# An attention stage: a weight tile's rounding and a gate's silu moved ahead by one pair of heads

## The chip, the cores and the metric

The kernel runs on one core of a Trainium2 chip. The metric is the device time of one execution in microseconds (us); lower is better. The time before is the median of three executions.

## The reference

The whole program is a model of several mixers and feed-forward layers over 512 tokens of width 1024. What the change touches is the attention stage of the last block. It has six pairs of heads of width 64: three pairs of "forgetting" attention (fox) and three pairs of indexer-selected attention (dsa). Cut to what matters:

```
z = rmsnorm(x) @ w_in                      # q, k, v and gate columns of each head
fox:  s = q.k * scale + F[t] - F[s], causal mask;    o = softmax(s) @ v;  out = o * silu(gate)
dsa:  s = q.k * scale over the top 128 keys of an indexer's score;  o = softmax(s) @ v;  out = o * silu(gate)
x = x + concat(mixers) @ w_out;  final rmsnorm
```

## The kernel before, in words

All work is done transposed: features lie on the partitions, 512 tokens along the free axis. A product in full precision is made of three matmuls on rounded parts: a weight tile is split into a high part (ScalarE, `split_high`, L151, 128x1024) and a low part (here GpSimd, `split_low`, L160), and TensorE multiplies high by high, low by high and high by low (L187 to L189).

`attention` (L2840) runs the six pairs i = 0 to 5 (NP = 6, of them NF = 3 fox). TensorE works on two pairs at once: while it attends over pair i it projects pair i + 1, which has four weight tiles s = 0 to 3 (queries, keys, gate, values), each of eight steps of three matmuls. The order is written out by hand, one program for each engine, and semaphores join them:

- **TensorE**, `body(i)` (L2945): the eight steps of tile 0 of the next pair, the turn (transpose) of the values (L204), `scores(i, 2)` (L2910), then for each of the eight items n (a head and a block of 128 queries; items 0 and 1 are the longest, with 512 keys) three more steps of the projection, the transposes of the probabilities `turn(i, n)` (L2918), scores of items to come at n = 1 and 3, and `values(i, n - 1)` (L2929). Tile 1 is steps 8 to 15, in items 0 to 2; tile 2 begins with step 16. Before the first step of a tile PE waits for that tile's low part and for its bank to be free. In the last pair PE does steps of the output projection (`mix`) in their place.
- **ScalarE (ACT)**, `body(i)` (L2986): `exp(n)` (L2992), `divide(n)` (L2997), the copy of the transposed probabilities out of PSUM, `turn(n)` (L3004), and between them the rounding of weight tiles of the next pair: `high(i + 1, 1)` after `divide(0)`, tiles 2 and 3 at n = 2 and 3, tile 0 of the pair after next at n = 4. The silu of the gate (L3017) stands between `divide(1)` and `turn(0)`, with a load of the silu table in front and of the exp table behind it (L3018). Its result lies in one buffer, `gate`, so it waits until the previous pair's output is formed.
- **VectorE (DVE)**, `body(i)` (L3083): per item the logits (L3099) and their maximum (L3101), the reciprocal of the sum of the item before (`invert`, L3076), in the fox pairs also a part of the choice of the 128 keys (L2826), and the takes of finished projections out of PSUM (`take`, L3071): queries at n = 1, keys at n = 3, gate at n = 6, values at the next pair's start. `out` (L3081) multiplies the gate into the previous pair's output at n = 1. In pair 4 it also makes the low parts of the output projection's sources (`half.low`, L554), one per item from n = 3.
- **GpSimd (POOL)** makes the low part of each weight tile as soon as the high one is there. **SyncE (SP)** loads a tile when the low part of the tile before in the same slot is done.

In what follows "pair 1" is the second pair, and the copy of item n is `turn(n)` on ACT.

Of the kernel before, what the change touches and what calls it, by code (L numbers as in the profile page):

```python
# [14 lines left out]
F32 = mybir.dt.float32  # L15
F32R = mybir.dt.float32r
U32 = mybir.dt.uint32
ACT = mybir.ActivationFunctionType
AX = mybir.AxisListType.X

P = 128
T = 512
# [30 lines left out]
LNEXP = "natural_log_exp_and_others"  # L53
# [33 lines left out]
class Core:  # L87
# [30 lines left out]
    def sb(self, name, shape, dtype=F32):  # L118
        return self.stack.enter_context(self.nc.sbuf_tensor(name, shape, dtype))

    def sem(self, name):
        self.sems.append(self.nc.alloc_semaphore(name))
        return self.sems[-1]
# [109 lines left out]
class Opening:  # L233
# [10 lines left out]
    def high(self, act, m, lo=0, hi=T):  # L244
        k = self.k
        k.nc.scalar.activation(k.uh[:, m, lo:hi], k.x[:, m, lo:hi], ACT.Copy, scale=self.gain(m)).then_inc(self.u_high, 1)
# [2593 lines left out]
def attention(k, fox_weights, dsa_weights, half):  # L2840
# [4 lines left out]
    nc = k.nc  # L2845
    sem, sb = k.sem, k.sb
    NF, NI = HF // 2, 2 * NT
    NP = 2 * NF
    R = 4
    items = [(a, t) for t in reversed(range(NT)) for a in range(2)]  # L2850
    qs, ks = ([sb(f"a_{s}{i}", [P, T], F32) for i in range(2)] for s in ("q", "k"))
    v, vraw, gate, graw = (sb(f"a_{s}", [P, T], F32) for s in ("v", "v_raw", "gate", "g_raw"))
    L = sb("a_logits", [P, R, T], F32)
    PT = sb("a_probsT", [P, 2, T], F32)
    st = sb("a_stats", [P, NI, 4], F32)
    taken = [sem(f"a_{s}_taken") for s in ("q", "k", "g", "v")]
# [4 lines left out]
    b_s, b_t, b_o = k.ps[4:6], k.ps[6], k.ps[7]  # L2861
# [4 lines left out]
    def y_tile(i):  # L2866

        return k.y[:, 5 + i if i < NF else 2 + i - NF, :]

    with nc.Block() as block:  # L2870
# [109 lines left out]
        @block.scalar  # L2980
        def _(act):
            def high(i, s):
                k.wait_product(act, 4 * i + s - 4)
                k.split_high(act, s, i)

            def body(i):  # L2986
                nxt2, end = i < NP - 1, i == NP - 1

                def exp(n):
                    act.wait_ge(max_ready, NI * i + n + 1)  # L2990
                    l = L[:, n % R, 0:(items[n][1] + 1) * P]
                    nc.scalar.activation(l, l, ACT.Exp, bias=st[:, n, 0:1], accum_out=st[:, n, 1:2]).then_inc(exp_done, 1)  # L2992

                def divide(n):
                    act.wait_ge(inverted, NI * i + n + 1)
                    l = L[:, n % R, 0:(items[n][1] + 1) * P]
                    nc.scalar.activation(l, l, ACT.Copy, scale=st[:, n, 2:3]).then_inc(p_ready, 1)  # L2997

                def turn(n):
                    t = items[n][1]  # L3000
                    act.wait_ge(turned, NI * i + n + 1)
                    if i or n >= 2:
                        act.wait_ge(pv_done, NI * i + n - 1)
                    nc.scalar.activation(PT[:, n % 2, 0:(t + 1) * P], b_t[:, 0:(t + 1) * P], ACT.Copy).then_inc(pt_ready, 1)  # L3004
                exp(0)
                exp(1)
                divide(0)
                high(i + 1, 1)
                act.wait_ge(v_turned, i + 1)
                if i:  # L3010
                    act.wait_ge(pv_done, NI * i)
                nc.scalar.activation(v[:, :], k.ps[3][:, :], ACT.Copy).then_inc(v_copied, 1)
                divide(1)
                act.wait_ge(taken[2], i + 1)
                if i:
                    act.wait_ge(y_ready, i)
                nc.scalar.activation(gate[:, :], graw[:, :], ACT.Silu).then_inc(gate_done, 1)  # L3017
                nc.scalar.preload_act_table_set(LNEXP)  # L3018
                turn(0)
                for n in range(2, NI):  # L3020
                    exp(n)
                    if n > 2:
                        divide(n - 1)
                    if n in (2, 3):
                        high(i + 1, n)
                    if nxt2 and n == 4:
                        high(i + 2, 0)
                    if i == NP - 2 and n < 7:
                        half.high(act, n - 2)
                    elif end and n in (2, 4):  # L3030
                        if n == 2:
                            k.wait_product(act, 4 * NP - 1)
                        half.high(act, 4 + n // 2)
                    elif end and n >= 6:
                        half.wait_product(act, n - 6)
                        half.split_high(act, n - 2)
                    if n > 2:
                        turn(n - 2)
                divide(NI - 1)
                turn(NI - 2)  # L3040
                turn(NI - 1)
                if end:
                    half.wait_product(act, 2)
                    half.split_high(act, 6)

            high(1, 0)
            for i in range(NP):
                body(i)
            act.wait_ge(y_ready, NP)
            half.high(act, KD - 1)  # L3050
# [9 lines left out]
        @block.vector  # L3060
        def _(dve):
            raws = (qs, ks, (graw, graw), (vraw, vraw))

            def take(i, s):

                k.wait_product(dve, 4 * i + s)
                if i and s == 2:
                    dve.wait_ge(gate_done, i)
                if i and s == 3:
                    dve.wait_ge(v_turned, i)  # L3070
                nc.vector.tensor_tensor(raws[s][i % 2][:, :], k.ps[s][:, :], k.rn[:, :], ALU.mult).then_inc(taken[s], 1)  # L3071

            def invert(i, n):

                dve.wait_ge(exp_done, NI * i + n + 1)
                nc.vector.reciprocal(st[:, n, 2:3], st[:, n, 1:2]).then_inc(inverted, 1)  # L3076

            def out(i):
                dve.wait_ge(pv_done, NI * i + NI)
                dve.wait_ge(gate_done, i + 1)  # L3080
                nc.vector.tensor_tensor(y_tile(i), gate[:, :], b_o[:, :], ALU.mult).then_inc(y_ready, 1)  # L3081

            def body(i):  # L3083
                end, fox = i == NP - 1, i < NF
                take(i, 3)
                if i == NF:
                    choice.finish(dve)
                for n, (a, t) in enumerate(items):
                    w, g = (t + 1) * P, NI * i + n
                    dve.wait_ge(st_done, g + 1)  # L3090
                    if g >= R:
                        dve.wait_ge(turned, g + 1 - R)
                    l = L[:, n % R, 0:w]
                    if fox:
                        d = b_s[a][:, w - P:w]
                        nc.vector.tensor_tensor(d, d, k.c("causal"), ALU.add).then_inc(masked, 1)
                        dve.wait_ge(masked, g + 1)
                    b = k.fb[:, 2 * i + a, 0:w] if fox else k.bias[:, OFF[t]:OFF[t + 1]]
                    nc.vector.scalar_tensor_tensor(l, b_s[a][:, 0:w], DH ** -0.5, b, ALU.mult, ALU.add).then_inc(logits_ready, 1)  # L3099
                    dve.wait_ge(logits_ready, g + 1)  # L3100
                    nc.vector.tensor_reduce(st[:, n, 0:1], l, AX, ALU.max, negate=True).then_inc(max_ready, 1)  # L3101
                    if fox:
                        choice.some(dve, 2)
                    if n:
                        invert(i, n - 1)
                    if n == 1 and i:
                        out(i - 1)
                    if fox:
                        choice.some(dve, 2)
                    if i < NP - 1 and n in (1, 3, 6):  # L3110
                        take(i + 1, (1, 3, 6).index(n))
                    if i == NP - 2 and n > 2:
                        half.low(dve, n - 3)
                    elif end and n in (3, 5):
                        half.low(dve, 4 + n // 2)
                invert(i, NI - 1)

            for s in range(3):
                take(0, s)
            for i in range(NP):  # L3120
                body(i)
            out(NP - 1)
            half.low(dve, KD - 1)
    k.count({s: NP for s in range(4)})
# [152 lines left out]
```

## Time and profile before

| | |
|---|---|
| median of 3 executions | 1842.07 us (1835.05 to 1844.43) |
| the profiled execution's own time | 1838.89 us |
| its span, first to last instruction | 1837.0 us |
| PE (matmuls) busy | 1741.9 us, 95% of the span |
| PEld (weight loads) busy | 1395.7 us, 76% |
| DVE busy | 1090.7 us, 59% |
| ACT busy | 854.3 us, 47% |
| POOL busy | 428.8 us, 23% |

The table shows where an engine spent its time over the whole program; the attention stage is the stretch from 1568 to 1810 us of the span. PE stands for the matmuls and PEld for the weight loads that go before them on the same engine. A row's idle time is the time in which the engine had nothing running in front of that instruction, with the instruction that ended the wait. Matmul ends are modelled, so successive matmuls overlap in the rows; a start is read directly.

### The profile page before, as it was taken

Reading aid. Unit: us, or ns where it says so; the run is one execution under the profiler, and the core shown is the slowest. Engines: PE = TensorE matmul, PEld = TensorE weight load, DVE = VectorE, ACT = ScalarE, POOL = GpSimd, SP = SyncE. Lnnn points to the kernel's source line nnn. Section 1 sums busy time; section 2 is a strip of 40 time slices with the busy share of each in tenths; the row PEclk is TensorE's granted clock in tenths of the full one; section 3 lists DMA queues with packets and bytes.
Section 4 is the critical chain, followed back from the end, with each engine's and each line's share of the span. In section 5 each row is a group of like instructions: output and inputs, shape, how many; then the busy total and the mean of one; then the engine's idle time right before and its main releaser. Section 6 shows DMA issues by size and latency. Waiting matters only on the chain. (4 is left out here: it accounts for less than half of the span.)

```text
span 1837.0 us, 23870 instructions
## 1 busy us (share of the span) xinstructions
PE 1741.9 (95%) x8346; PEld 1395.7 (76%) x8346; DVE 1090.7 (59%) x1705; ACT 854.3 (47%) x1452; POOL 428.8 (23%) x332
## 2 busy tenths in 40 slices
PE   7998998999999999899999999999999989899997
PEld 5666887777888888777888877888888766666665
DVE  5544444567565643678788848666553476667243
ACT  5553455544333332456555645333332352445663
POOL 0342454211111100135546510111100111222222
PEclk9999999999999999999999999999999999999999
DMA  5111100232223222311222121322232320211121
GB/s 206 38 69 58 47 35 24 75 109 72 100 93 101 92 93 101 103 47 58 69 69 69 48 92 58 102 93 95 76 115 98 108 74 22 80 47 46 58 69 46
DMA packets 39904, 140.28 MB, mean 76 GB/s; under 512 B 4496, under 2 KB 4752, under 8 KB 39696
## 3 DMA queue, kind: packets, MB, share of 16 engines
q1 hardware_dynamic: 39824, 139.23, 22.5%
q8 instruction: 49, 0.80, 0.2%
q14 instruction: 31, 0.25, 0.0%
HBM read 137.11 MB, written 2.10 MB: 76 GB/s over the span
## 5 line engine op out<-in xcount | busy, mean ns | idle before, releaser
L187 PE MATMUL bank<-u_high,w_high 128*128 128x512 f32 x1580 | 650.4, 412 | 24.2 <-POOL w_low L160 9.9
L189 PE MATMUL bank<-u_high,w_low 128*128 128x512 f32 x1580 | 621.5, 393 | 0.0
L188 PE MATMUL bank<-u_low,w_high 128*128 128x512 f32 x1580 | 620.9, 393 | 0.0
L187 PEld LDWEIGHTS bank<-u_high,w_high 128*128 128x128 f32 x1580 | 300.5, 190 | 113.8 <-issue 37.5
L151 ACT ACTIVATE w_high<-w_ring 128x1024 fp32r<-128x1024 f32 x233 | 244.1, 1052 | 226.3 <-PE bank L189 172.7
L189 PEld LDWEIGHTS bank<-u_high,w_low 128*128 128x128 f32 x1580 | 299.3, 189 | 65.5
L188 PEld LDWEIGHTS bank<-u_low,w_high 128*128 128x128 f32 x1580 | 300.8, 190 | 58.3 <-issue 3.8
L160 DVE TENSOR_TENSOR w_low<-w_ring,w_high 128x1024 fp32r<-128x1024 f32 x176 | 221.0, 1258 | 178.9 <-ACT w_high L151 178.7
L160 POOL TENSOR_TENSOR w_low<-w_ring,w_high 128x1024 fp32r<-128x1024 f32 x57 | 135.7, 2390 | 544.3 <-ACT w_high L151 544.3
L881 ACT ACTIVATE conv_up<-bank,col_sb 128x512 f32<-128x512 f32 x88 | 68.6, 780 | 270.5 <-DVE bank L936 270.5
L996 POOL TENSOR_TENSOR hidden<-conv_up 128x512 f32 x44 | 58.2, 1323 | 494.0 <-DVE conv_up L947 373.7
L936 DVE TENSOR_TENSOR bank<-bank,root_in 128x512 f32<-128x512 f32 x88 | 61.4, 698 | 134.1 <-PE bank L189 133.5
L187 PE MATMUL bank<-src_high_down,w_high 128*128 128x512 f32 x352 | 137.3, 390 | 2.3 <-DVE src_low_down L479 2.3
L188 PE MATMUL bank<-src_low_down,w_high 128*128 128x512 f32 x352 | 136.9, 389 | 0.0
L189 PE MATMUL bank<-src_high_down,w_low 128*128 128x512 f32 x352 | 136.9, 389 | 0.0
L1319 POOL TENSOR_TENSOR c_X<-c_k,c_dif 128x256 f32<-128x256 f32 x56 | 59.4, 1060 | 149.9 <-ACT c_dif L1210 149.9
L187 PEld LDWEIGHTS bank<-src_high_down,w_high 128*128 128x128 f32 x352 | 66.1, 188 | 17.5 <-issue 2.2
L189 PEld LDWEIGHTS bank<-src_high_down,w_low 128*128 128x128 f32 x352 | 66.1, 188 | 13.7
L188 PEld LDWEIGHTS bank<-src_low_down,w_high 128*128 128x128 f32 x352 | 66.1, 188 | 13.6
L946 DVE SCALAR_TENSOR_TENSOR conv_up<-bank,col_sb,conv_up 128x511 f32<-128x511 f32 x88 | 65.9, 749 | 15.6 <-ACT conv_up L881 11.9
L947 DVE SCALAR_TENSOR_TENSOR conv_up<-bank,col_sb,conv_up 128x510 f32<-128x510 f32 x88 | 65.9, 748 | 10.1 <-DVE conv_up L946 0.3
L1354 DVE TENSOR_TENSOR c_dif<-c_G 128x512 f32<-128x512 f32 x56 | 54.5, 997 | 24.9 <-PE bank L1116 24.5
(414 smaller groups left out, 2320.8 us busy)
## 6 DMA issues: line engine op xcount, KB each, us to landing
w_ring<-ffn_up SPq DMA_DIRECT2D x88, 512.0 KB, 3.4
w_ring<-ffn_down SPq DMA_DIRECT2D x44, 512.0 KB, 3.4
w_ring<-c_in SPq DMA_DIRECT2D x32, 512.0 KB, 3.4
w_ring<-g_in SPq DMA_DIRECT2D x16, 512.0 KB, 3.9
w_ring<-m_in SPq DMA_DIRECT2D x12, 512.0 KB, 4.9
w_ring<-fox_in SPq DMA_DIRECT2D x12, 512.0 KB, 3.5
w_ring<-dsa_in SPq DMA_DIRECT2D x12, 512.0 KB, 3.4
w_ring<-ab_out SPq DMA_DIRECT2D x8, 512.0 KB, 4.7
```

The lines of the kernel that those rows point to most:

```text
L151: self.nc.scalar.activation(self.ws[s][0][:, :], self.w[:, s, :], ACT.Copy).then_inc(self.w_high, 1)
L160: eng.tensor_tensor(low[:, :], self.w[:, s, :], high[:, :].bitcast(F32), ALU.subtract).then_inc(self.w_split, 1)
L187: nc.tensor.matmul(out, a[0], b[0], start=start, stop=False)
L188: nc.tensor.matmul(out, a[0], b[1], start=False, stop=False)
L189: return nc.tensor.matmul(out, a[1], b[0], start=False, stop=stop)
L881: nc.scalar.activation(cg[:, s, :], bank(i, s)[:, :], ACT.Identity, bias=coef(4 * i + s, 3), scale=coef(4 * i + s, 2)).then_inc(tap_done, 1)
L936: nc.vector.tensor_tensor(bank(i, s)[:, :], bank(i, s)[:, :], k.rn[:, :], ALU.mult).then_inc(taken, 1)
L946: ch.link(nc.vector.scalar_tensor_tensor(cg[:, s, 1:T], bank(i, s)[:, 0:T - 1], coef(4 * i + s, 1), cg[:, s, 1:T], ALU.mult, ALU.add))
L947: nc.vector.scalar_tensor_tensor(cg[:, s, 2:T], bank(i, s)[:, 0:T - 2], coef(4 * i + s, 0), cg[:, s, 2:T], ALU.mult, ALU.add).then_inc(con ...
L996: nc.gpsimd.tensor_tensor(h[:, bass.ds(2 * i + s // 2, 1), :], cg[:, s - 1:s, :], cg[:, s:s + 1, :], ALU.mult).then_inc(mul_done, 1)
L1319: nc.gpsimd.tensor_tensor(x[:, :, 0, :], blocks(kk[:, :], b)[:, :, 0, :], d[:, :, 0, :], ALU.mult)
L1354: nc.vector.tensor_tensor(dif[:, l % R, :].rearrange("p (n b) -> p n b", b=2 * b), g, ref, ALU.subtract).then_inc(diff_ready, 1)
```

## The change

- ACT rounds tile 1 of the pair after next at n = 5, in the pair in front (`high(i + 2, 1)`), in place of `high(i + 1, 1)` in the pair itself; tile 1 of pair 1 is rounded before the loop. POOL and SP follow in the same order of tiles.
- The gate has two buffers. The silu of pair i + 1 with its two table loads stands at the end of pair i on ACT, behind the last copy; that of pair 0 before the loop.
- DVE takes the next pair's keys at n = 4 and not at n = 3.
- In pair 4 DVE's low parts begin at n = 4; the fifth follows the fourth at n = 7.

```diff
--- before.py
+++ after.py
@@ -2849,7 +2849,8 @@
     R = 4
     items = [(a, t) for t in reversed(range(NT)) for a in range(2)]
     qs, ks = ([sb(f"a_{s}{i}", [P, T], F32) for i in range(2)] for s in ("q", "k"))
-    v, vraw, gate, graw = (sb(f"a_{s}", [P, T], F32) for s in ("v", "v_raw", "gate", "g_raw"))
+    v, vraw, graw = (sb(f"a_{s}", [P, T], F32) for s in ("v", "v_raw", "g_raw"))
+    gates = [sb(f"a_gate{i}", [P, T], F32) for i in range(2)]
     L = sb("a_logits", [P, R, T], F32)
     PT = sb("a_probsT", [P, 2, T], F32)
     st = sb("a_stats", [P, NI, 4], F32)
@@ -2983,6 +2984,13 @@
                 k.wait_product(act, 4 * i + s - 4)
                 k.split_high(act, s, i)
 
+            def silu(i):
+                act.wait_ge(taken[2], i + 1)
+                if i > 1:
+                    act.wait_ge(y_ready, i - 1)
+                nc.scalar.activation(gates[i % 2][:, :], graw[:, :], ACT.Silu).then_inc(gate_done, 1)
+                nc.scalar.preload_act_table_set(LNEXP)
+
             def body(i):
                 nxt2, end = i < NP - 1, i == NP - 1
 
@@ -3005,17 +3013,11 @@
                 exp(0)
                 exp(1)
                 divide(0)
-                high(i + 1, 1)
                 act.wait_ge(v_turned, i + 1)
                 if i:
                     act.wait_ge(pv_done, NI * i)
                 nc.scalar.activation(v[:, :], k.ps[3][:, :], ACT.Copy).then_inc(v_copied, 1)
                 divide(1)
-                act.wait_ge(taken[2], i + 1)
-                if i:
-                    act.wait_ge(y_ready, i)
-                nc.scalar.activation(gate[:, :], graw[:, :], ACT.Silu).then_inc(gate_done, 1)
-                nc.scalar.preload_act_table_set(LNEXP)
                 turn(0)
                 for n in range(2, NI):
                     exp(n)
@@ -3023,8 +3025,8 @@
                         divide(n - 1)
                     if n in (2, 3):
                         high(i + 1, n)
-                    if nxt2 and n == 4:
-                        high(i + 2, 0)
+                    if nxt2 and n in (4, 5):
+                        high(i + 2, n - 4)
                     if i == NP - 2 and n < 7:
                         half.high(act, n - 2)
                     elif end and n in (2, 4):
@@ -3039,11 +3041,15 @@
                 divide(NI - 1)
                 turn(NI - 2)
                 turn(NI - 1)
+                if nxt2:
+                    silu(i + 1)
                 if end:
                     half.wait_product(act, 2)
                     half.split_high(act, 6)
 
             high(1, 0)
+            high(1, 1)
+            silu(0)
             for i in range(NP):
                 body(i)
             act.wait_ge(y_ready, NP)
@@ -3078,7 +3084,7 @@
             def out(i):
                 dve.wait_ge(pv_done, NI * i + NI)
                 dve.wait_ge(gate_done, i + 1)
-                nc.vector.tensor_tensor(y_tile(i), gate[:, :], b_o[:, :], ALU.mult).then_inc(y_ready, 1)
+                nc.vector.tensor_tensor(y_tile(i), gates[i % 2][:, :], b_o[:, :], ALU.mult).then_inc(y_ready, 1)
 
             def body(i):
                 end, fox = i == NP - 1, i < NF
@@ -3107,10 +3113,12 @@
                         out(i - 1)
                     if fox:
                         choice.some(dve, 2)
-                    if i < NP - 1 and n in (1, 3, 6):
-                        take(i + 1, (1, 3, 6).index(n))
-                    if i == NP - 2 and n > 2:
-                        half.low(dve, n - 3)
+                    if i < NP - 1 and n in (1, 4, 6):
+                        take(i + 1, (1, 4, 6).index(n))
+                    if i == NP - 2 and n > 3:
+                        half.low(dve, n - 4)
+                        if n == 7:
+                            half.low(dve, n - 3)
                     elif end and n in (3, 5):
                         half.low(dve, 4 + n // 2)
                 invert(i, NI - 1)
```

## Rows read from the trace of the kernel before

**Rows 1.** Windows, pair by pair from one scores(i, 2) to the next.
```profile
core 0: us, PE busy (x) PEld busy (x) DVE busy (x) ACT busy (x) POOL busy (x), PEclk, DMA share, GB/s
1579.99:1618.31 38.32, 35.20 (x177) 25.33 (x177) 27.49 (x82) 18.32 (x38) 9.38 (x4) 1.00 0.17 55
1618.31:1657.52 39.21, 35.18 (x178) 25.33 (x177) 29.19 (x87) 19.82 (x41) 9.44 (x4) 1.00 0.16 55
1657.52:1697.78 40.26, 36.21 (x177) 26.61 (x176) 27.62 (x80) 21.37 (x42) 10.25 (x5) 0.96 0.16 53
1697.78:1733.97 36.19, 34.99 (x177) 25.40 (x176) 11.43 (x30) 19.38 (x40) 9.83 (x5) 1.00 0.19 59
1733.97:1771.39 37.42, 34.02 (x171) 24.12 (x171) 17.54 (x34) 21.78 (x45) 8.31 (x4) 1.00 0.16 57
...
```

**Rows 2.** Waits of the stage: who for whom, us in total, times, longest.
```profile
PEld bank L187 <- POOL w_low L160: 15.6, 10, 3.9
...
DVE a_k L3071 <- PE bank L189: 14.3, 5, 3.5
...
PE bank L187 <- POOL w_low L160: 9.2, 6, 3.3
...
PE bank L2918 <- ACT a_probsT L3004: 7.4, 10, 1.9
```

**Rows 3.** Timeline of PE in pair 1: start, us, instruction, count [idle before it].
```profile
1618.31 0.92 PE L2910 MATMUL bank<-a_k,a_q 64*128 64x384 f32 x4
1622.51 0.50 PE L187 MATMUL bank<-u_high,w_high 128*128 128x512 f32 x1 [3.28 <-POOL w_low L160]
...
1624.71 0.60 PE L2918 MATMUL bank<-cst_sb,a_logits 128*128 128x128 f32 x4
...
1627.90 0.63 PE L2918 MATMUL bank<-cst_sb,a_logits 128*128 128x128 f32 x4 [0.50 <-ACT a_probsT L3004]
...
1631.82 0.51 PE L187 MATMUL bank<-u_high,w_high 128*128 128x512 f32 x1
...
1636.59 0.52 PE L2918 MATMUL bank<-cst_sb,a_logits 128*128 128x128 f32 x3 [0.19 <-ACT a_probsT L3004]
```

**Rows 4.** Timeline of ACT in pair 1.
```profile
1623.18 0.72 ACT L2997 ACTIVATE a_logits<-a_logits,a_stats 128x512 f32<-128x512 f32 x1 [2.67 <-DVE a_stats L3076]
...
1625.22 0.63 ACT L3017 ACTIVATE a_gate<-a_g_raw 128x512 f32<-128x512 f32 x1
1625.87 1.28 ACT L3018 ACT_TABLE_LOAD   x1
1627.16 0.60 ACT L3004 ACTIVATE a_probsT<-bank 128x512 f32<-128x512 f32 x1
...
1628.25 1.04 ACT L151 ACTIVATE w_high<-w_ring 128x1024 fp32r<-128x1024 f32 x1
```

**Rows 5.** Timeline of POOL (one row) and DVE in pair 1.
```profile
1620.11 2.35 POOL L160 TENSOR_TENSOR w_low<-w_ring,w_high 128x1024 fp32r<-128x1024 f32 x1 [20.84 <-ACT w_high L151]
...
1631.80 0.69 DVE L3071 TENSOR_TENSOR a_k<-bank,root_in 128x512 f32<-128x512 f32 x1 [2.08 <-PE bank L189]
```

**Rows 6.** Timeline of ACT where pairs meet: 1 to 2, and 3 to 4.
```profile
1652.92 0.72 ACT L2992 ACTIVATE a_logits<-a_logits,a_stats 128x512 f32<-128x512 f32 x1 [2.56 <-DVE a_stats L3101]
...
1729.01 0.73 ACT L2992 ACTIVATE a_logits<-a_logits,a_stats 128x512 f32<-128x512 f32 x1 [2.22 <-DVE a_stats L3101]
```

**Rows 7.** Timeline of POOL, DVE, ACT and PE in pair 4.
```profile
1744.95 2.37 POOL L160 TENSOR_TENSOR w_low<-w_ring,w_high 128x1024 fp32r<-128x1024 f32 x1 [0.18 <-ACT w_high L151]
...
1745.40 2.46 DVE L554 TENSOR_TENSOR mix_low<-y_mix,mix_high 128x512 fp32r<-128x512 f32 x1
...
1748.68 0.51 ACT L2992 ACTIVATE a_logits<-a_logits,a_stats 128x256 f32<-128x256 f32 x1 [2.81 <-DVE a_stats L3101]
...
1751.78 0.52 PE L2918 MATMUL bank<-cst_sb,a_logits 128*128 128x128 f32 x3 [1.95 <-ACT a_probsT L3004]
```

**Rows 8.** Windows, four us behind the longest wait, in pair 2.
```profile
1660.00:1664.00 4.00, 2.25 (x5) 1.82 (x6) 3.86 (x12) 1.76 (x2) 1.70 (x1) 0.71 0.28 97
```


## The prediction

> **What bounds the kernel.** The page gives PE 95% of the span, so I went to the stage that the change touches and cut it into pairs [rows 1]. From one `scores(i, 2)` to the next the first three pairs, fox, take 38.3, 39.2 and 40.3 us, and the next, dsa, 36.2, though PE is busy for about 35 us in each. PE sets the time, and what exceeds 35 us is mostly waits. The list of waits says which [rows 2]: matmuls waited 9.2 us in all, six times, for a weight tile's low part, and the transposes 7.4 us, ten times, for the copy of the item before out of PSUM. That is 16.6 us in a stage of 242.
>
> The timelines of pair 1 show where the two are made [rows 3 to 5]. PE ends its scores at 1619.2 and stands 3.28 us before step 8, because tile 1 was rounded by ACT only after `divide(0)`; POOL's part, 2.35 us, ended at 1622.46. The first copy (1627.16) stands behind the second divide and the gate's block, 1623.90 to 1627.16: a silu of 0.63 and two table loads of 1.28. Its transposes for item 1 waited for it 0.50 us more. The third piece is in pair 4 [rows 7]: a transpose waits 1.95 us, because ACT came late to `exp(4)` (2.81 us idle); the maximum before it stood on DVE behind the keys, for which DVE waits 14.3 us in five pairs [rows 2].
>
> **The change, part by part.**
>
> *Tile 1 a pair earlier.* Its 1.04 us on ACT [rows 4] and 2.35 us on POOL are done some 20 us before PE wants them: POOL had been idle for 20.84 us in front of that work [rows 5], so it has room. SP's load for the slot also goes out earlier. Step 8 then waits for nothing: the 9.2 us go. What ACT gains at the start of a pair it pays at n = 5, 1.04 us between `divide(4)` and the copy of item 3. The third part pays for that.
>
> *The gate's block.* 3.26 us leave the way of the first copy. In pair 1 that copy can start at 1623.18 + 0.67 = 1623.85, since `divide(1)` is held by DVE and not by PE [rows 4]. PE gets to it like this [rows 3]: scores end at 1619.2, three steps last 2.2 (1622.51 to 1624.71), the transposes and three steps more 2.7 (1624.71 to 1627.40), so it is there at 1624.1, and the copy ends near 1624.5. So about 0.4 us of wait stays in pair 1, and by the same path about 0.2 in pair 2. From the copy to step 16 lies a chain of exp, rounding of tile 2 and POOL's 2.35: 1627.16 to 1631.82, 4.66 us. It now starts at 1623.85 and ends at 1628.5, where PE would come at 1628.0. So step 16 is 3.3 us earlier than before, and not 3.8. In a dsa pair DVE has no choice of keys to make (busy 11.4 us against 27 to 29 [rows 1]), and I find no wait there.
>
> The block itself now stands between the last copy of a pair and the next `exp(0)`, where ACT had idled 2.56 us between pairs 1 and 2 and 2.22 us between pairs 3 and 4 [rows 6]. 3.26 us is more: `exp(0)` comes 0.7 and 1.0 us late. PE meets item 0 first in its transposes, some 9 us later, and the second exp had idle time in front of it, so I cost this at nothing. Were that cover gone, it would be at most 1.0 us in each of five pairs, 5 us. The number of table loads is as before.
>
> *Keys one item later.* DVE no longer waits for them in front of the fourth item's maximum. In pair 4 `exp(4)`, at 1748.68, loses its 2.81 of idleness and some 2.3 of the gate's block (there PE's transposes of item 0 end last) and stands near 1743.6; the copy of item 2, which let PE go at 1751.78, 3.1 later, comes by 1746.7 [rows 7]. PE's own way from `scores(i, 2)` to that place is, in pair 1, 0.9 + 2.2 + 2.7, then 3.4 to step 16 (3.92 less the wait of 0.5) and 4.6 to the transposes of item 3 (1631.82 to 1636.40) [rows 3]: 13.8, here from 1733.97 to 1747.8. So the 1.95 goes, and the smaller waits of its kind in pairs 0 to 2 with it. At n = 4 DVE may wait a little for the keys, whose product ends in step 15; item 5's logits are needed by PE after those 4.6 us, against 1.5 us of work on DVE.
>
> *The low parts of pair 4.* One took 2.46 us, from 1745.40 to 1747.86, nearly to the end of POOL's split beside it (1744.95 + 2.37 = 1747.32) [rows 7]; a piece of this size (128x512) takes DVE 0.69 when it takes the keys [rows 5]. Each that meets POOL costs up to 2.46 - 0.69 = 1.8 us more. POOL has one more split in the second half of the pair, so up to two low parts may meet it. I count nothing, since PE does not read them before pair 5. The Trainium skill (SBUF — State Buffer, "SBUF: two separate sides") says that a DVE operation with two SBUF inputs and a GpSimd operation that reads SBUF shut each other out for a whole instruction. By it the moved split would block one more low part, and the sum would be poorer by 1.8 us at most; the row agrees with the rule for this operation.
>
> *Sum.* Gone are 9.2 + 7.4. Left are 0.4 + 0.2 of the first copies' waits, and 0.6 at step 16 in the fox pairs. Four of the ten PEld waits for low parts were of tile 2, 0.5 us each, and cost PE about 0.3 each beyond its own pace, which the PE rows do not count; three go, 0.9. In pair 2 PE was granted 0.71 of its clock in the four us behind the longest wait [rows 8], half the rate (1.2 GHz) in a part of them, and its busy time is 1.0 us over that of pairs 0 and 1 [rows 1]; that goes with the wait. 9.2 + 7.4 - 0.6 - 0.6 + 0.9 + 1.0 = 17.3 us. The Trainium skill (TensorE: Matmul & The Clock Gate, part 1) says that the clock falls after idleness and that when it does so is not tied to the kernel; two waits of equal length differ here as it says (pair 1 kept its clock). By that rule the 1.0 would be anything from 0 to about 3, by which of the three waits were hit.
>
> The profiled execution took 1838.9 us and becomes 1821.6; the median stands 3.2 us above it, and against that I forecast 1842.1 - 17.3 = **1824.8 us**.
>
> **The rivals.**
>
> *DVE keeps the fox pairs.* DVE is busy 27 to 29 us there [rows 1], in nearly unbroken order from the scores to `invert(1)`, and ACT's `divide(1)` waited 2.67 us for it [rows 4]. The margins that I found are 0.4 to 1 us. If DVE runs late by 2 us in each fox pair, PE waits for copies or scores what it now waits for weights: 3 x 2 = 6 us less, and with the 1.0 of late `exp(0)` in two pairs 8 less. Gain 9 to 11, time about 1832. For it: the tight margins; against: DVE itself is released earlier at `exp(2)` and the keys.
>
> *Slower: the keys' wait moved in front of item 5.* DVE's wait for the keys, up to 3.3 us and 2.9 in the mean [rows 2], now stands before the logits of item 5, and ACT has 1.04 us more between `divide(4)` and the copy of item 3. If DVE waits for the keys at n = 4 as long as it did at n = 3, that copy is late by 3.3 + 0.7 + 1.0 = 5.0 us, of which I count 1.5 as slack before PE's transposes of item 4; 3.5 x 5 = 17.5 us. The waits of 7.4 would also stay, as they'd only change their item, and the gain would be 9.2 + 1.0. Time 1842 + 17.5 - 10.2 = about 1849. It decides where DVE comes to the keys over 1.5 us before step 15 is done. Against it: item 4's work alone fills about 2 us, and PE comes earlier by the waits removed.
>
> *Little: the weights alone.* The gate's block at the pair's end holds `exp(0)` and by it the whole chain of items, so that of the 7.4 nothing is won, and five times 1.0 is lost: 9.2 + 1.0 - 5.0 = 5.2, time 1837. Against it speaks that the second exp waited for DVE after the first. That the change does not do what it says can be only in tile 1's load coming late; SP waits only for a split that is then a pair earlier.
>
> **Chances.** Forecast 0.70, DVE in the fox pairs 0.15, weights alone 0.09, slower 0.06. What a measurement of this kernel can tell from no change is about 0.5%, 9.2 us. The forecast's own bounds are a gain of 13 (late `exp(0)` in three pairs) to 20 (clock, by rows 1 and 8); runs of one kernel here differ by 9 us, so a median may be off by 3 to 4. The range of 8 in 10 goes from 1842.1 - 20 - 4 = 1818 to the second case's 1832 with the same 4, 1836. Faster takes the forecast and two thirds of the DVE case, with a little lost to scatter: 0.79. The same is the rest of it and most of the weights' case: 0.15; slower 0.06.
>
> **What would show it.** In the changed kernel's list of waits, PE for low parts in the stage should be under 1 us and for copies under 1.5; the fox pairs should take 35 to 36 us each; the wait of `exp(0)` in front of pairs should be gone, and no transpose of item 4 should wait. Wrong would be: fox pairs at 37 or more, DVE's wait for `a_k` still near 14 us, or waits of `scores(i, 4)` and `scores(i, 6)` for logits.

## The result, and the profile after

The changed kernel takes 1818.2 us (median of 4, 1815.1 to 1819.6) against 1839.7 for the kernel before (4 runs): a ratio of 0.9882, 95% interval [0.9863, 0.9902], that is 1.2% or 18 to 25 us faster. A second measurement of the same pair on another occasion gave 0.9879 [0.9863, 0.9896]. The span went from 1837.0 to 1815.8 us, by 21.2. The forecast was a gain of 17.3, below the interval. The forecast time was 1824.8 us, 6.6 above the measured one; 2.4 of that is the kernel before, whose median was 1839.7 here and 1842.1 in the forecast, and 4.2 is the gain.

The windows of the changed kernel, again from one `scores(i, 2)` to the next (they answer to [rows 1]):

```profile
core 0: us, PE busy (x) PEld busy (x) DVE busy (x) ACT busy (x) POOL busy (x), PEclk, DMA share, GB/s
1578.87:1613.30 34.43, 34.43 (x177) 25.56 (x176) 27.30 (x82) 19.31 (x39) 9.53 (x4) 1.00 0.19 62
1613.30:1648.77 35.47, 34.92 (x178) 25.41 (x177) 29.01 (x87) 19.71 (x41) 9.53 (x4) 1.00 0.18 61
1648.77:1684.09 35.32, 34.97 (x178) 25.40 (x177) 27.53 (x80) 20.32 (x41) 9.56 (x4) 1.00 0.19 60
1684.09:1718.60 34.51, 34.51 (x177) 25.54 (x176) 11.65 (x30) 19.39 (x40) 9.44 (x4) 1.00 0.19 62
1718.60:1751.75 33.15, 33.15 (x171) 24.43 (x170) 16.39 (x34) 21.88 (x45) 9.57 (x4) 1.00 0.19 64
```

The pairs took 38.3, 39.2, 40.3, 36.2 and 37.4 us and take 34.4, 35.5, 35.3, 34.5 and 33.2. In pairs 0, 3 and 4 PE is busy for the whole stretch, and the clock is full in all five. From the first `scores(0, 2)` to the end of the span there were 257.0 us (1837.0 - 1579.99) and are now 236.9 (1815.8 - 1578.87): 20.1 of the 21.2 us come from the stage. The rest lies in front of it, where nothing was changed; from profile to profile of the kernels below, `scores(0, 2)` begins anywhere between 1575.6 and 1584.2. I therefore compare stages in what follows and give the timed ratios beside them.

The waits of the stage after the change (they answer to [rows 2]: 14.3, 9.2 and 7.4 us before):

```profile
DVE a_k L3077 <- PE bank L189: 3.4, 2, 1.7
...
PE bank L187 <- POOL w_low L160: 1.0, 1, 1.0
PE bank L2919 <- ACT a_probsT L3012: 0.8, 2, 0.5
```

The one wait for a low part in this list is at the stage's entry, before the first step of all, and is no rest of the 9.2 us: from the entry's scores to that first step there were 2.16 us before and are 2.17 now, but in the kernel before the scores' row lasted 2.08 us, at a lower clock, and left no idle time to list.

What ACT does where pairs 1 and 2 meet (it answers to [rows 6]); behind the last copy stands the gate's block, then `exp(0)` at once, and `exp(1)` still has 2.11 us of idleness in front of it:

```profile
1641.32 0.28 ACT L3012 ACTIVATE a_probsT<-bank 128x128 f32<-128x128 f32 x1 [2.69 <-PE bank L2919]
1641.62 1.28 ACT L2991 ACT_TABLE_LOAD   x1
1642.91 0.63 ACT L2991 ACTIVATE a_gate<-a_g_raw 128x512 f32<-128x512 f32 x1
1643.56 1.28 ACT L2992 ACT_TABLE_LOAD   x1
1644.86 0.73 ACT L3000 ACTIVATE a_logits<-a_logits,a_stats 128x512 f32<-128x512 f32 x1
1645.49 0.18 ACT L3000 ACTIVATION_READ_ACCUMULATOR a_logits<-a_logits,a_stats 128x1 f32 x1
1647.78 0.72 ACT L3000 ACTIVATE a_logits<-a_logits,a_stats 128x512 f32<-128x512 f32 x1 [2.11 <-DVE a_stats L3107]
```

To see where the time came from, I took the starts of PE's weight loads at the same places in both traces. A start is read and not modelled. Sums over the six pairs, in us:

| from, to | before | after | won |
|---|---|---|---|
| `scores(i, 2)` to step 8 | 14.4 | 5.1 | 9.3 |
| step 8 to the transposes of item 1 | 34.2 | 28.5 | 5.8 |
| those to the transposes of item 2 | 27.6 | 26.6 | 1.0 |
| those to the transposes of item 3 | 26.3 | 21.7 | 4.6 |
| the rest of the stage, nearly all of it between the transposes of items 3 and 4 | | | -0.7 |
| stage | 257.0 | 236.9 | 20.1 |

### The profile page after: what moved, and what is told of

It reads as the page before. It is cut to its first block and busy times, and to the rows that moved or that the text cites. A ratio compares the mean times of both kernels' runs of the same rounds, so it can differ in the third digit from the quotient of the medians.

```text
span 1815.8 us, 23867 instructions
## 1 busy us (share of the span) xinstructions
PE 1736.1 (96%) x8346; PEld 1396.6 (77%) x8346; DVE 1089.1 (60%) x1705; ACT 851.8 (47%) x1450; POOL 429.7 (24%) x332
```

## The experiments

Theory 1 is that of the forecast's sum: each part of the change has a price of its own, the waits that it takes away. Theory 2 is a series: the waits stand beside one another, so that a part alone uncovers the next one, and only the three together pay. The first six kernels are the three parts alone and in twos. Results, each against the kernel before; a stage figure is that of one profiled execution, with what the clock did in it, and differs from the timed one by up to 4 us:

| parts in the kernel | timed ratio, 95% interval | stage, us |
|---|---|---|
| tile 1 | 1.0028 [1.0017, 1.0039] | +5.2 |
| gate | 0.9983 [0.9972, 0.9993] | -4.4 |
| keys | 0.9984 [0.9970, 0.9999] | -4.0 |
| gate and keys | 0.9948 [0.9931, 0.9964] | -7.8 |
| tile 1 and keys | 0.9984 [0.9974, 0.9993] | +0.9 |
| tile 1 and gate | 0.9905 [0.9888, 0.9921] | -16.2 |
| all three | 0.9882 [0.9863, 0.9902] | -20.1 |

Read in pairs of rows, the table separates the parts. The keys are worth 3.4 to 4.3 us whichever of the others are there. Tile 1 costs 5.2 and 4.9 us where the gate's block is in its old place, and wins 11.8 and 12.3 where it is moved; the gate wins about 4 without tile 1 and 21 with it. The series is thus one of tile 1 and the gate's block; for the keys the sum theory holds.

**Tile 1 alone.**

```diff
                 divide(0)
-                high(i + 1, 1)
...
-                    if nxt2 and n == 4:
-                        high(i + 2, 0)
+                    if nxt2 and n in (4, 5):
+                        high(i + 2, n - 4)
...
             high(1, 0)
+            high(1, 1)
```

> Series theory: the wait for tile 1 lies beside the gate's block. In pair 1 of the kernel before the first copy ends 9.4 us after scores(i, 2), held by DVE's reciprocal and the gate's block, and PE with no wait for tile 1 would be at the transposes of item 1 after 5.3 us; so it waits there for what it no longer waits in front of step 8, and the time moves by less than 2 us against before. Sum theory (the forecast's): the 9.2 us of waits for low parts go, 9 us faster than before.

It is slower than before, by 0.28% or 5 us, where the series theory allowed less than 2. The kernel's waits:

```profile
DVE a_k L3071 <- PE bank L189: 18.0, 5, 4.0
PE bank L2918 <- ACT a_probsT L3004: 17.9, 11, 3.8
...
PE bank L187 <- POOL w_low L160: 1.0, 1, 1.0
```

The matmuls' 9.2 us of waits for low parts are gone (the 1.0 is the one at the entry), and the transposes' wait for copies rose from 7.4 to 17.9: the whole of it went over, and 1.3 us more. In pair 1 the timelines of ACT and of PE show how:

```profile
1623.05 0.72 ACT L2997 ACTIVATE a_logits<-a_logits,a_stats 128x512 f32<-128x512 f32 x1 [3.61 <-DVE a_stats L3076]
...
1627.03 0.60 ACT L3004 ACTIVATE a_probsT<-bank 128x512 f32<-128x512 f32 x1
```

```profile
1627.77 0.63 PE L2918 MATMUL bank<-cst_sb,a_logits 128*128 128x128 f32 x4 [3.84 <-ACT a_probsT L3004]
```

The second divide starts where it did, 4.86 us behind the scores (1618.19; before, 4.87 [rows 3, 4]), now after an idleness of 3.61 us, because DVE's reciprocal sets it; the gate's block follows, the copy stands at 1627.03, and PE, which is there 3.3 us sooner, waits for it. One wait of 3.84 us took the place of two of 3.28 and 0.50 [rows 3]. Behind it the windows show a fallen clock, where the kernel before had 1.00 in that pair:

```profile
1626.00:1630.00 4.00, 2.23 (x13) 1.76 (x14) 1.51 (x6) 3.99 (x8) 0.76 (x1) 0.87 0.00 0
1630.00:1634.00 4.00, 4.00 (x17) 3.06 (x15) 0.78 (x2) 1.70 (x3) 3.96 (x2) 0.71 0.33 106
```

From item 1's transposes to item 2's there are 5.8 us in all three fox pairs, against 4.4 to 4.5 before, 3.9 us in all. In pair 4 the clock fell once more (0.65 from 1754 to 1758 us), and item 4's transposes came 5.19 us behind item 3's in place of 3.65. That is 5.4 us of clock, against the 1.5 that the kernel before loses in pair 2; of the stage's 5.2 us the clock thus makes 3.9 and the waits alone 1.3, within what the series theory allowed. DVE now waits 18.0 us for the keys. Theory 1 is out for this part.

**The gate alone** (the changed kernel with tile 1 and the keys as before).

```diff
                 divide(0)
+                high(i + 1, 1)
...
-                    if nxt2 and n in (4, 5):
-                        high(i + 2, n - 4)
+                    if nxt2 and n == 4:
+                        high(i + 2, 0)
...
-            high(1, 1)
...
-                    if i < NP - 1 and n in (1, 4, 6):
-                        take(i + 1, (1, 4, 6).index(n))
+                    if i < NP - 1 and n in (1, 3, 6):
+                        take(i + 1, (1, 3, 6).index(n))
```

> Series theory: step 8 keeps its wait, and the transposes of item 1 come 4.5 us behind step 8 in place of 5.3 to 6.0, so that about 0.8 to 1.5 us are won in each of six pairs, and some more at item 3: 6 to 9 us faster than before. Sum theory: the copies' waits alone, 5 to 7 us faster.

3 us timed, 4.4 in the stage: less than either theory gave. Its waits:

```profile
DVE a_k L3077 <- PE bank L189: 18.1, 5, 4.4
...
PE bank L187 <- POOL w_low L160: 10.5, 7, 3.3
...
PE bank L2919 <- ACT a_probsT L3012: 3.8, 4, 1.6
```

From step 8 to item 2's transposes 5.2 us are won. But from item 2 to item 3 nothing is (27.1 us against 26.3): what comes before it is earlier, so DVE waits longer for the keys (18.1 us against 14.3), in front of the next maximum. And the wait in front of step 8 now drops the clock in pairs 1 and 2 (3.3 and 3.1 us from step 8 to item 0's transposes, against 2.0 at full clock); in the kernel before it did so in pair 2 alone (3.5 us).

**The keys alone.**

```diff
-                    if i < NP - 1 and n in (1, 3, 6):
-                        take(i + 1, (1, 3, 6).index(n))
-                    if i == NP - 2 and n > 2:
-                        half.low(dve, n - 3)
+                    if i < NP - 1 and n in (1, 4, 6):
+                        take(i + 1, (1, 4, 6).index(n))
+                    if i == NP - 2 and n > 3:
+                        half.low(dve, n - 4)
+                        if n == 7:
+                            half.low(dve, n - 3)
```

> Both theories: the transposes of item 3 lose the 4.6 us by which they came late in pairs 0 to 4 (start to start from item 2), 3 to 5 us faster than before; DVE's wait for the keys falls from 14.3 us to under 5. If the whole of the 4.6 stems from the gate's block, which makes ACT late at all items after it, the gain is under 1 us.

As expected: 4.0 in the stage, 0.16% timed, and item 3's transposes come 3.4 to 3.6 us behind item 2's in every pair. This part does have a price of its own. The wait in front of step 8 is still there, and the clock fell at it in pairs 1 and 2 (0.66 from 1624 to 1628 us and 0.57 from 1666 to 1670), so that the whole gain is less than the 4.9 us between items 2 and 3.

**All but tile 1** and **all but the keys** (the edits above, undone in the changed kernel).

> The changed kernel with tile 1 rounded in its own pair again. Both theories: the waits in front of step 8 (9.4 us start to start) come back in full, since no other wait covers them now: 9 to 10 us slower than the changed kernel, about 11 faster than before.

> The changed kernel with the keys taken at n = 3 and the low parts of pair 4 as before. Series theory and sum theory: the waits of item 3's transposes come back, 3 to 5 us slower than the changed kernel. If they stemmed from the gate's block, which is still away, under 1 us slower.

Without tile 1 the time is 0.66% above the changed kernel's ratio, 12 us, more than expected. Its waits for low parts are those of before, with the 1.0 of the entry in the list as well:

```profile
PE bank L187 <- POOL w_low L160: 10.4, 7, 3.3
```

Start to start they make 9.6 us; the other 3 are the clock, which fell behind that wait in pairs 1 and 2 (3.0 and 3.6 us in place of 2.0, and the stretch behind it 3.1 and 3.6 in place of 2.5). Without the keys' move it is 4 us slower (0.9905 against 0.9882), and item 3's waits are back, so they do not stem from the gate's block.

**All but the gate.**

```diff
                 divide(1)
+                silu(i)
                 turn(0)
...
-                if nxt2:
-                    silu(i + 1)
...
-            silu(0)
```

> The changed kernel with the silu between the second divide and the first copy again. Series theory: the first copy is late by 3.26 us again, and in the fox pairs PE has no other wait that hides it, so the waits of tile 1 come back under another name: 14 to 17 us slower than the changed kernel, 4 to 6 faster than before. Sum theory: only the copies' waits come back, 5 to 7 us slower than the changed kernel.

The plainest verdict for the series: 21 us come back in the stage, 19 by the timed ratios, where the sum theory gave 5 to 7 and the series theory 14 to 17. Tile 1's wait is away and the keys are out of the way, but the copies' wait is 13.8 us, and the clock in pair 1 falls to near half (1.2 GHz) in the eight us from 1626 on, as the long wait ends. The waits, then the windows of pair 1:

```profile
PE bank L2919 <- ACT a_probsT L3012: 13.8, 7, 3.8
```

```profile
1626.00:1630.00 4.00, 2.31 (x9) 1.36 (x10) 1.46 (x7) 3.99 (x8) 0.84 (x1) 0.59 0.02 4
1630.00:1634.00 4.00, 4.00 (x14) 3.28 (x15) 2.94 (x9) 3.63 (x7) 4.00 (x3) 0.56 0.29 98
```

**Is the block free where it now stands?** A second silu, of 64 columns into a spare buffer, and two more table loads were put in front of it.

```diff
             def silu(i):
                 act.wait_ge(taken[2], i + 1)
...
+                if i:
+                    nc.scalar.activation(spare[:, :], graw[:, 0:64], ACT.Silu)
+                    nc.scalar.preload_act_table_set(LNEXP)
                 nc.scalar.activation(gates[i % 2][:, :], graw[:, :], ACT.Silu).then_inc(gate_done, 1)
```

> The changed kernel with a second silu (of 64 columns, into a spare buffer) and two more table loads in front of the gate's block where pairs meet, about 2.9 us of ACT in each of five pairs. If the block costs nothing there (the forecast), exp(0) has a further slack of over 2 us and the time is the same within 1.5 us in the fox pairs' cover; if its place is on the path, 5 x 2.9 = 14 us slower. I expect 0 to 3 us slower, from the dsa pairs, where exp(1) and divide(0) stand close to the copy of the values.

Within the interval it is free: 0.9883 [0.9867, 0.9900] against before, like the changed kernel, and the five pair lengths are the same as in the windows above to 0.02 us, though `exp(0)` came 2.8 us later. The cover does have an end: in the last pair PE needs the values at its first steps of the output projection, and there it waited 2.02 us for them, on a copy that stands behind the doubled block and both exps (PE's timeline):

```profile
1754.79 0.92 PE L2912 MATMUL bank<-a_k,a_q 64*128 64x384 f32 x4
1757.72 0.50 PE L187 MATMUL bank<-mix_high,w_high 128*128 128x512 f32 x1 [2.02 <-ACT a_v L3023]
```

That stretch, from `scores(5, 2)` to the end, is 3.6 us longer in this profile, clock included; the profiled execution was the longest of the four (1824.6 us, the others 1819.0 to 1819.8), so it need not be as much in the others.

**Four attempts to win more, beside a repetition of the changed kernel.** First DVE's reciprocal in front of the key choice at n = 2:

```diff
+                    if n == 2:
+                        invert(i, 1)
                     if fox:
                         choice.some(dve, 2)
-                    if n:
+                    if n and n != 2:
                         invert(i, n - 1)
```

> The changed kernel beside the three that follow: 1.2% faster than before, 20 to 23 us.

> The changed kernel with DVE's reciprocal of item 1 moved in front of the two steps of the key choice at n = 2. In the changed kernel the transposes of item 1 come 3.36 and 3.18 us behind those of item 0 in pairs 1 and 2, against 2.52 where nothing is waited for. If that wait is DVE's chain to the reciprocal (series theory), both become 2.5 and 1.5 us are won. If it is ACT's own work, nothing is won.

The repetition gave 0.9879, this one 0.9860 [0.9844, 0.9876]; the intervals overlap, and the stage is 0.9 us shorter. The transposes of item 1 did go to 2.52 us in both pairs, so the wait was DVE's chain. Of the 1.5 us won there 0.6 came back at once: PE now waits for the logits of item 3, on the same engine (PEld's timeline of pair 1),

```profile
1621.26 0.30 PEld L2911 LDWEIGHTS bank<-a_k,a_q 64*128 64x128 f32 x4 [0.53 <-DVE a_logits L3105]
```

and for tile 2; from item 1 to item 2 are 4.90 and 5.12 us in place of 4.53 and 4.54.

Then the last values product of a pair was put behind the first step of the next:

```diff
-                    project(i + 1, 0, 8)
+                    project(i + 1, 0, 1)
...
+                if i:
+                    values(i - 1, NI - 1)
+                if nxt:
+                    project(i + 1, 1, 8)
...
-                values(i, NI - 1)
+                if not nxt:
+                    values(i, NI - 1)
```

> The changed kernel with the last values product of a pair put behind the first projection step of the next, so that PE does not stand 0.76 us for the last copy (five times in the trace). One step lasts 0.7 us: about 0.6 x 5 = 3 us won, if nothing else in the pair's start waits for that product.

> Both edits: 4 to 5 us faster than the changed kernel, about 26 faster than before.

Both missed: 0.9886 [0.9869, 0.9902] and 0.9881 [0.9864, 0.9897], and clean pairs are 0.54 us longer (35.05 against 34.51). The weight loads at the meeting of pairs 3 and 4 show the misreading, with the matmuls of the same place under them:

```profile
1709.13 0.30 PEld L2911 LDWEIGHTS bank<-a_k,a_q 64*128 64x128 f32 x4 [0.29 <-issue]
1710.18 0.19 PEld L2930 LDWEIGHTS bank<-a_probsT,a_v 128*64 128x64 f32 x2 [0.76 <-ACT a_probsT L3019]
1710.55 0.19 PEld L187 LDWEIGHTS bank<-u_high,w_high 128*128 128x128 f32 x1 [0.17 <-issue]
...
1711.45 0.19 PEld L2930 LDWEIGHTS bank<-a_probsT,a_v 128*64 128x64 f32 x2 [0.37 <-issue]
```

```profile
1709.13 1.13 PE L2911 MATMUL bank<-a_k,a_q 64*128 64x512 f32 x4
1710.19 0.43 PE L2930 MATMUL bank<-a_probsT,a_v 128*64 128x128 f32 x2
```

The 0.76 us that the row puts down to ACT's copy are still there, now in front of the product of item 6: the weight loader stands idle because the matmuls of the scores run for 1.13 us beside it. It was no wait, and the split product only pays a second gap of 0.37 before it.

Last, two steps of the choice went from n = 2 to n = 7, and ACT rounded tile 2 in its idle time in front of the second divide:

```diff
                 nc.scalar.activation(v[:, :], k.ps[3][:, :], ACT.Copy).then_inc(v_copied, 1)
+                high(i + 1, 2)
                 divide(1)
...
-                    if n in (2, 3):
+                    if n == 3:
...
-                    if fox:
-                        choice.some(dve, 2)
+                    if fox and n != 2:
+                        choice.some(dve, 2 if n < NI - 1 else 4)
```

> The changed kernel with three things together: DVE makes two of the key choice's steps at n = 7 and not at n = 2, in front of the reciprocal of item 1; ACT rounds tile 2 in its idle time in front of the second divide. With the reciprocal alone moved, the wait of item 1's transposes in pairs 1 and 2 went (2.52 us from item 0's) but came back in part as waits for item 3's logits and tile 2 (4.90 and 5.12 us from item 1's to item 2's transposes, against 4.38). If these are the next two links of the same series, both go now, the fox pairs take 34.5 us like the others, and the stage is 1.7 to 1.9 us shorter than the changed kernel's; the time is about 1.3% under before. If DVE's work at n = 7 delays the next pair's start, nothing is won over the changed kernel.

0.9877 [0.9861, 0.9894], the changed kernel's time; the stage is 1.2 us shorter over the five pairs. Both waits went (2.50 to 2.53 and 4.37 to 4.39 us in all pairs), but item 6's transposes came 0.2 to 0.6 us later in the fox pairs. None of the four is told apart from the changed kernel by its time.

## Why the forecast was right in kind and too small

- *Tile 1, 9.2 us, and step 8 waiting for nothing*: right for the whole change (9.3 start to start). It was right only because the gate's block went as well: alone this part costs 5 us. The forecast's text priced the parts one by one and its third rival gave the weights alone a gain; that is refuted, and no row of the list of waits could show it. The sign was there in [rows 4]: the copy that follows the wait was not late because of tile 1.
- *The copies, 7.4 less 0.6*: **this is the term that failed**. By the starts of the loads, against the same stretch where nothing is waited for (2.52, 4.38 and 3.61 us in the changed kernel), the ten waits of 7.4 were 10.8 us, and 1.5 are left, so that 9.3 were won and not 6.8. The idle time in a matmul's row starts at the modelled end of the matmul before it, and ends are modelled late: a start follows 0.23 us after the last, while the row lasts 0.39. So each such row is some 0.2 to 0.4 us short, ten times. In the changed kernel the transposes of item 1 in pair 1 show it, in PE's timeline first and in that of its loads second:

```profile
1613.30 0.92 PE L2911 MATMUL bank<-a_k,a_q 64*128 64x384 f32 x4
1614.15 0.50 PE L187 MATMUL bank<-u_high,w_high 128*128 128x512 f32 x1
...
1619.52 0.63 PE L2919 MATMUL bank<-cst_sb,a_logits 128*128 128x128 f32 x4 [0.47 <-ACT a_probsT L3012]
```

```profile
1616.13 0.59 PEld L2919 LDWEIGHTS bank<-cst_sb,a_logits 128*128 128x128 f32 x4
...
1619.49 0.42 PEld L2919 LDWEIGHTS bank<-cst_sb,a_logits 128*128 128x128 f32 x4 [0.88 <-ACT a_logits L3005]
```

  The first says 0.47, the second 0.88; from 1616.13 to 1619.49 are 3.36 us, where pairs without a wait have 2.52, so 0.84 is the price. In pair 4 before, the row of 1.95 [rows 7] was 2.16 from start to start (5.77 us from item 2's transposes to item 3's, now 3.61).
- *Residual waits in pairs 1 and 2, 0.4 and 0.2 us*: both there, 0.84 and 0.66 by starts, 0.47 and 0.29 by rows. DVE's chain was named rightly (moving the reciprocal took them away). The 0.6 at step 16 was 0.15 in each of the two pairs, 0.3, too dear by half.
- *The weight loads' waits for tile 2, 0.9*: too dear as well. The four of them cost PE 0.14 us each, not 0.3 (4.52 us from item 1's transposes to item 2's against 4.38), 0.6 in all, of which 0.3 is left at step 16. That this term and the last still made the right 0.3 together is luck.
- *The clock, 1.0 us*: gone, and the stage now runs at 1.00 from pair 0 on. By the starts it was 1.5 (3.46 us from step 8 to item 0's transposes in pair 2, 1.98 now). The stage's 20.1 us are then 9.3 for step 8, 9.3 for the copies, 1.5 for the clock, 0.3 for tile 2 and 0.4 in the last pair, less 0.7 behind item 3. What the forecast said of the Trainium skill's rule (TensorE: Matmul & The Clock Gate, part 1), that the same wait may or may not be hit, bore out: waits of 3.3 us in front of step 8, in pairs 1 and 2, brought the clock down in one of two in the kernel before, and in both in the kernels with the gate alone (0.62 and 0.58 in the four us behind them), with the keys alone and with all but tile 1 (0.58 and 0.50).
- *The block's new place costs nothing*: right, with a margin of more than 2.8 us except in the last pair.
- *Keys*: DVE's wait went from 14.3 to 3.4 us, and item 3's waits went with it, in every pair.
- *Low parts that meet POOL*: two did, 1.35 and 2.18 us, no more than in the kernel before (2.46 and 2.44), and PE noticed neither (DVE's timeline of pair 4):

```profile
1728.67 1.35 DVE L554 TENSOR_TENSOR mix_low<-y_mix,mix_high 128x512 fp32r<-128x512 f32 x1
...
1730.80 2.18 DVE L554 TENSOR_TENSOR mix_low<-y_mix,mix_high 128x512 fp32r<-128x512 f32 x1
```

- *Rivals*: fox pairs at 37 us, the keys' wait moved to item 5, and the weights alone did not occur. The range's lower end, 1818, was the measured time itself: that end was taken from the clock and from scatter, and held no error of the waits' sizes.

Not settled: the timed gain exceeds the stage's by about 1 us, which I put down to scatter in front of the stage and did not test.

## What to carry to other kernels

Read the cost of a wait between the starts of two fixed places, with and without it, and not from the idle time of the row. Before a wait is priced, ask what the waiting engine would meet next if it were gone: here the weight's wait, removed alone, made the kernel 5 us slower, and with the gate's block moved as well the two gave 16 us; the keys, on which neither depended, added 4. A block that must be somewhere (a silu with its two table loads) belongs in the engine's longest idle stretch, and a second buffer is the price for putting it there.

## What the runs showed of the hardware

- Waits of 2.5 to 3.8 us of TensorE, in front of the transposes in the fox pairs, were each followed by a fallen clock: in the two kernels with tile 1 moved and the gate's block in its old place, a window of four us behind the wait was granted 0.50 to 0.77 in all six cases, and such a pair lost 1.2 to 2.5 us between item 1's and item 2's transposes. Waits of 3.3 us in front of step 8 were followed by one in seven of eight cases (four kernels, pairs 1 and 2). The eighth is pair 1 of the kernel before, at 1.00, with its waits of 3.3 and 0.5. Whether a wait in two pieces is safer is thus not shown.
- The weight loader's idle time beside long matmuls is put down to whatever semaphore came last: 0.76 us five times a stage, none of it a wait.
